# Building both long-convolution filters ahead of the projections of a one-core diffusion step, with their norm folded into the short convolution

## The reference, cut to what matters

```python
def _hyena_spectrum(n, w1, b1, w2, b2, w3, b3, freq):
    ...
    h = jnp.sin(fr * (z @ w1.astype(f32) + b1.astype(f32)))
    h = jnp.sin(fr * (h @ w2.astype(f32) + b2.astype(f32)))
    h = (h @ w3.astype(f32) + b3.astype(f32)).reshape(n, HY_ORDER, 2, HY_DIM)
    ...
    h = h * jnp.exp(-t01[:, None] * deltas[None, :])[:, None, None, :]
    ...
    filt2n = jnp.concatenate([h_fwd, jnp.zeros((1, HY_ORDER, HY_DIM), f32), h_bwd[:0:-1]], axis=0)
    filt2n = filt2n * lax.rsqrt(jnp.sum(filt2n * filt2n, axis=0, keepdims=True) + EPS)
    return jnp.fft.rfft(filt2n, axis=0)

def _hyena(u, conv_w, conv_b, spec, bias):
    n = u.shape[1]
    uc = _short_conv3(u, conv_w, conv_b)
    v, x1, x2 = jnp.split(uc, HY_ORDER + 1, axis=-1)
    ...
        return y + b_o.astype(jnp.float32) * zf
    z = x1.astype(jnp.float32) * long_conv(v, spec[:, 0], bias[0])
    z = x2.astype(jnp.float32) * long_conv(z, spec[:, 1], bias[1])
    return z.astype(u.dtype)
```

## Time and profile before

| what | value |
|---|---|
| runs | 928.21, 933.62, 936.93 us, median 933.62 |
| span of the profiled execution | 936.8 us (first to last instruction), 0.1 below the highest run |
| TensorE busy | 815.2 us, 87% |
| VectorE, ScalarE, GpSimd busy | 379.1, 272.2, 108.8 us |
| mean granted TensorE clock | 0.927 |
| input projection starts, `uT` ends | 75.3 us, 187.3 us |

### The profile page before, as it was taken

The page is one execution under the profiler, slowest core; times in us unless marked ns, Lnnn a source line. Parts: engine busy times, 40 slices in busy tenths (PEclk is TensorE's granted clock), DMA queues, the critical chain, the costliest instruction groups (busy, mean ns, idle before and its releaser), DMA issues.

```text
span 936.8 us, 11642 instructions
## 1 busy us (share of the span) xinstructions
PE 815.2 (87%) x4091; PEld 455.8 (49%) x4091; DVE 379.1 (40%) x848; ACT 272.2 (29%) x636; POOL 108.8 (12%) x161
## 2 busy tenths in 40 slices
PE   4779999999888996999977699988889998999860
PEld 0236665544443464555535346555554565555430
DVE  3366583265164143332111544654651432322114
ACT  1241212121451142122211536564540332222111
POOL 2300000000000003100013002202200022010120
PEclk9879999999988996899999799889999967999995
DMA  9991222259982246999997966202109378999965
GB/s 268 369 340 38 82 90 97 90 180 342 267 344 75 105 155 252 326 408 410 411 348 246 352 219 251 89 4 92 48 1 349 135 265 299 405 410 410 379 246 205
DMA packets 84559, 220.17 MB, mean 235 GB/s; under 512 B 9636, under 2 KB 19549, under 8 KB 84185
## 3 DMA queue, kind: packets, MB, share of 16 engines
q1 hardware_dynamic: 73570, 197.04, 58.3%
q0 software_dynamic: 9120, 18.75, 5.9%
q10 hardware_dynamic: 1816, 3.68, 1.1%
HBM read 214.77 MB, written 14.89 MB: 245 GB/s over the span
## 4 chain that ended last, share of the span: by engine, by line
PE 65%; DMA 15%; DVE 7%; ACT 4%; issue 4%; SPq 3%; DVEq 1%; POOLq 1%; POOL 0%; ACTq 0%
PE ps L903 58%; PE ps L910 4%; DMA ring<-in_moe_w_up_dram 3%; DMA ring<-in_w_mod_dram 2%; PE ps L1130 2%; DMA arena<-in_moe_w_up_dram 2%; DMA y_rows<-arena,ck 2%; SPq L643 2%; DMA xn<-y_rows 1%; DVEq L1877 1%; SPq L660 1%; DMA h_rows<-xn 1%; DMA hT<-h_rows,rows_in 1%; DVE negmax L1930 1%; ACT hT L1598 1%
## 5 line engine op out<-in xcount | busy, mean ns | idle before, releaser
L903 PE MATMUL ps<-arena 128*64 128x256 f32 (+12 forms) x1164 | 244.0, 455 | 26.2 <-DMA arena<-in_moe_w_up_dram 7.1
L903 PEld LDWEIGHTS ps<-arena 128*64 128x64 f32 (+4 forms) x1164 | 131.9, 172 | 119.2 <-issue 72.0
L903 PE MATMUL ps<-ring,hT 128*128 128x512 f32 (+2 forms) x384 | 134.1, 509 | 4.5 <-issue 3.9
L903 PE MATMUL ps<-ring,arena 128*64 128x256 f32 (+1 forms) x784 | 111.3, 431 | 4.8 <-DMA ring<-in_moe_w_down_dram 3.6
L903 PEld LDWEIGHTS ps<-ring,hT 128*128 128x128 f32 x384 | 73.3, 193 | 63.2 <-issue 58.8
L903 PEld LDWEIGHTS ps<-ring,arena 128*64 128x64 f32 x784 | 53.8, 137 | 50.6 <-issue 27.8
L910 PE MATMUL ps<-ident,arena 128*128 128x128 f32 (+2 forms) x332 | 52.3, 300 | 15.4 <-DVE hT L1936 3.6
L1554 ACT ACTIVATE arena<-ps 128x256 f32<-128x256 f32 (+4 forms) x88 | 38.5, 453 | 89.0 <-PE ps L903 84.9
L903 PE MATMUL ps<-hT,ring 128*128 128x384 f32 x192 | 62.1, 486 | 0.0
L2262 DVE TENSOR_TENSOR arena<-arena,ps 128x128 f32<-128x128 f32 x37 | 10.6, 287 | 125.3 <-ACT arena L1660 125.3
L903 PE MATMUL ps<-ring,condT 128*32 128x512 f32 x384 | 52.9, 676 | 9.7 <-DMA ring<-in_w_mod_dram 9.0
(11 more groups left out here) (299 smaller groups left out, 878.6 us busy)
## 6 DMA issues: line engine op xcount, KB each, us to landing
ring<-in_w_mod_dram SPq DMA_DIRECT2D x48, 1024.0 KB, 8.3
ring<-in_moe_w_down_dram SPq DMA_DIRECT2D x22, 1024.0 KB, 16.2
ring<-in_moe_w_gate_dram SPq DMA_DIRECT2D x38, 512.0 KB, 12.9
ring<-in_moe_w_up_dram SPq DMA_DIRECT2D x38, 512.0 KB, 15.1
arena<-in_moe_w_gate_dram SPq DMA_DIRECT2D x36, 512.0 KB, 8.7
arena<-in_moe_w_up_dram SPq DMA_DIRECT2D x36, 512.0 KB, 9.7
arena<-in_moe_w_down_dram SPq DMA_DIRECT2D x15, 1024.0 KB, 10.9
ring<-in_ev_w_in_dram SPq DMA_DIRECT2D x9, 1024.0 KB, 13.2
```

What stands on the lines that cost most here:

```text
L903: mm = pe.matmul(out, lhsT, rhs, **kw)
```

## The change

Both filters are built before chunk 2, and the steps that follow are put ahead of x's transposes. The scale 1/root is no longer put on the spectrum. The first filter's goes into the coefficients of the short convolution of v, the second's into those of x1, per channel and token group; for this the roots are transposed to channels on partitions (`root_turn`). The skip term becomes a tap: root times bias is added to row 0 of the filter before its transform (`bias_taps`). The energies have 32 output rows in place of 128, in one bank, the context's in one column group and the latents' in another. The four loads of the filter network's first layer go from ScalarE's queue to the head of SyncE's; the decay table is sent before piece 2 in place of piece 4, and the skip term is loaded for one partition in place of 128.

```diff
@@ banks
     B.stage("filt3.0", 2 * NT)
+    B.stage("filt3.1", 2 * NT)
     mod_stage("start", 2)
+    B.stage("energy0", 1)
+    B.stage("rootT0", 1)
+    B.stage("spec0", 2 * NT)
     mod_stage("start", 3)
-    B.stage("energy0", 2)
+    B.stage("energy1", 1)
+    B.stage("rootT1", 1)
+    B.stage("spec1", 2 * NT)
+    B.stage("convT", 1)
     B.stage("hT0.0", 6)
...
@@ buffers
-        filt = view(6144, NT, 2, HY)
+        filt = [view(6144, NT, 2, HY), view(16896, NT, 2, HY)]
...
+        raw = [flat_hT[:, D * (1 + i):D * (2 + i)].rearrange("p (r n) -> p r n", r=2) for i in range(2)]
@@ SyncE
                 if i == 0:
+                    load(sp, in_filt, zT, d["zT"])
+                    load(sp, in_filt, filtc[0:EMB, 3 + HID:3 + 2 * HID], d["ev_filt_w1"][0])
+                    load(sp, in_filt, filtc[:, 0:1], d["ev_filt_b1"].rearrange("a n -> n a"))
+                    load(sp, in_filt, filtc[:, 2:3], d["ev_filt_freq"].rearrange("a n -> n a"))
...
-                if i == 4:
                     load(sp, in_filt3, decay, d["decay"].rearrange("p (a b) -> p a b", b=HY))
-                    load(sp, in_filt3, hybias[:, 0, :], d["ev_hy_bias"][0, 0].partition_broadcast(P))
-                    load(sp, in_filt3, hybias[:, 1, :], d["ev_hy_bias"][0, 1].partition_broadcast(P))
+                    load(sp, in_filt3, hybias[0:1, :, :], d["ev_hy_bias"])
@@ TensorE
             def spectrum(od):
-                pe.wait_ge(esq_ready, (od + 1) * NT)
+                pe.wait_ge(tap_ready, od + 1)
...
+                bank = claim(f"energy{od}")
+                for t, r in ((0, 0), (1, 0), (0, 1), (1, 1), (2, 0), (2, 1)):
+                    pe.wait_ge(esq_ready, od * NT + max(t, 1) + 1)
+                    g = GRP[t]
+                    mm = product(bank[32 * g:32 * g + 32, :], onesm[:, 0:32], sqs[:, t, r, :], start=t < 2 and r == 0, stop=t != 1 and r == 1)
+                fill_inc(mm, f"energy{od}")
+
+            def root_turn(od):
+                pe.wait_ge(root_ready, od + 1)
+                bank = claim(f"rootT{od}")
+                for g in range(2):
+                    for c in range(NCH):
+                        at_col = 32 * (NCH * g + c)
+                        mm = pe.transpose(bank[:, at_col:at_col + 32], energy_root[od][:, g, c * P:(c + 1) * P], ident[0:32, 0:32])
+                fill_inc(mm, f"rootT{od}")
...
             filters(0)
-            for i in (2, 3, 4):
-                mod_step("start", i)
+            filters(1)
+            mod_step("start", 2)
             energies(0)
             loaded(pe, in_mod)
-            for t in range(NT):
-                mixer_turn(0, t)
+            root_turn(0)
             loaded(pe, in_dft)
             spectrum(0)
+            for i in (3, 4):
+                mod_step("start", i)
+            energies(1)
+            root_turn(1)
+            spectrum(1)
             bank = claim("convT")
...
+            for t in range(NT):
+                mixer_turn(0, t)
             for i in range(6):
                 drained_wait(pe, "hT0.0", i)
             for q in (6, 7, 8, 0, 1, 2, 3, 4, 5):
-                if q == 7:
-                    filters(1)
-                if q == 8:
-                    energies(1)
-                    spectrum(1)
-                if q == 0:
-                    pe.wait_ge(spec_done, 12)
@@ ScalarE
             def energy_roots(od):
+                bank = filled_wait(act, f"energy{od}")
                 for g in range(2):
-                    act.wait_ge(eroot, 2 * od + g + 1)
-                    act.activation(esc[:, g, :], esc[:, g, :], ACT.Sqrt).then_inc(escale_ready, 1)
+                    ins = act.activation(energy_root[od][:, g, :], bank[32 * g:32 * g + 32, :], ACT.Sqrt, bias=eps_col[0:32, :], scale=0.5)
+                drain_inc(ins, f"energy{od}")
+                act.drain().then_inc(root_ready, 1)
+
+            def spectrum_copies(od):
+                for i in (2, 4, 0):
+                    copy_out(f"spec{od}", i, H[:, od, i % 2, i // 2, :], bank_of(f"spec{od}", i)[:, :])
...
+            mod_step("start", 2)
+            energy_roots(0)
+            for t in range(NT):
+                filter_squares(1, t)
+            spectrum_copies(0)
+            mod_step("start", 3)
+            energy_roots(1)
             loaded(act, in_x)
             for t in range(NT):
                 norm_tile(0, t)
-            energy_roots(0)
+            spectrum_copies(1)
...
+                if m < 2 * NCH:
+                    for g, (a, b) in enumerate(((0, NPR), (NPR, T))):
+                        act.activation(uc[:, m, a:b], bank[:, a:b], ACT.Identity, bias=conv_scaled[:, g, 3, m:m + 1], scale=conv_scaled[:, g, 1, m:m + 1])
@@ VectorE
+            def bias_taps(od):
+
+                dve.wait_ge(root_ready, od + 1)
+                tap = raw[0][0:1, :, :]
+                dve.tensor_tensor(tap, energy_root[od][0:1, :, :], hybias[0:1, od, :].unsqueeze(1).broadcast_to([1, 2, HY]), ALU.mult)
+                settle()
+                first = filt[od][0:1, 0:2, 0, :]
+                dve.tensor_tensor(first, first, tap, ALU.add).then_inc(tap_ready, 1)
...
             filters(0)
+            filters(1)
+            bias_taps(0)
+            root_inverse(0)
+            for i in range(1, 3):
+                mod_step("start", i)
+            spectrum_copies(0)
+            bias_taps(1)
+            root_inverse(1)
             norm(0)
-            energies(0)
-            for i in range(1, 5):
-                mod_step("start", i)
+            mod_step("start", 3)
+            spectrum_copies(1)
+            mod_step("start", 4)
             for t in range(NT):
                 modulate_tile(0, 0, t, "hT0.0", 2 * t + 1)
-            spectrum(0)
...
-            filters(1)
-            energies(1)
-            spectrum(1)
```

More of the change, by code:

```diff
@@ L450, in build_step @@
         convraw = view(15360, P, parts=48)
-        esc = view(15488, 2, HY)
+        energy_root = [view(15488, 2, HY, parts=32), view(13312, 2, HY, parts=32)]
         hidden = view(16512, T, parts=HID + 1)
@@ L1288, in spectrum @@
                         for k in range(2):
-                            mm = product(bank[:, :], dfts[:, r, k, ft * P:(ft + 1) * P], filt[:, 1 + k, r, :],
+                            mm = product(bank[:, :], dfts[:, r, k, ft * P:(ft + 1) * P], filt[od][:, 1 + k, r, :],
                                            start=k == 0, stop=k == 1)
@@ L1293, in spectrum @@
                     bank = claim(f"spec{od}", r)
-                    mm = product(bank[:, :], dftp[:, r, :], filt[:, 0, r, :], start=True, stop=True)
+                    mm = product(bank[:, :], dftp[:, r, :], filt[od][:, 0, r, :], start=True, stop=True)
                     fill_inc(mm, f"spec{od}", r)
@@ L1782, in _ @@
                 modulate_tile(0, 0, t, "hT0.0", 2 * t)
-            heads_copy(0)
-            for t in range(NT):
-                filter_squares(1, t)
-            heads_copy(1)
-            energy_roots(1)
-            heads_copy(2)
+            for q in range(3):
+                heads_copy(q)
             act.wait_ge(qvar, 1)
@@ L2386, in energies @@
-            def energies(od):
-                for g in range(2):
-                    bank = filled_wait(dve, f"energy{od}", g)
-                    drain_inc(dve.tensor_scalar(esc[:, g, :], bank[:, :], 0.5, EPS, ALU.mult, ALU.add), f"energy{od}", g)
-                    dve.drain().then_inc(eroot, 1)
-            def spectrum(od):
-                for g in range(2):
-                    dve.wait_ge(escale_ready, 2 * od + g + 1)
-                    dve.reciprocal(esc[:, g, :], esc[:, g, :])
-                settle()
-                for i in range(2 * NT):
-                    ft, r = i // 2, i % 2
-                    bank = filled_wait(dve, f"spec{od}", i)
-                    ins = dve.tensor_tensor(H[:, od, r, ft, :], bank[:, :], esc[:, GRP[ft], :], ALU.mult)
-                    drain_inc(ins, f"spec{od}", i)
-                settle()
-                for ft in range(NT):
-                    dve.tensor_tensor(H[:, od, 0, ft, :], H[:, od, 0, ft, :], hybias[:, od, :], ALU.add)
-                dve.drain().then_inc(spec_done, 6)
@@ new lines, in root_inverse, with spectrum_copies @@
+            def root_inverse(od):
+                bank = filled_wait(dve, f"rootT{od}")
+                first = bank[:, 0:8 * 32].rearrange("p (g c k) -> p g c k", g=2, c=NCH)[:, :, :, 0]
+                drain_inc(dve.reciprocal(inv_root_c[:, :, NCH * od:NCH * od + NCH], first), f"rootT{od}")
+            def spectrum_copies(od):
+                for i in (3, 5, 1):
+                    bank = filled_wait(dve, f"spec{od}", i)
+                    drain_inc(dve.tensor_copy(H[:, od, i % 2, i // 2, :], bank[:, :]), f"spec{od}", i)
@@ L2413, in _ @@
                 modulate_tile(0, 0, t, "hT0.0", 2 * t + 1)
-            spectrum(0)
             bank = filled_wait(dve, "convT")
```

(4 more changed lines are left out.)

61 lines of the change are left out of this document (27 added, 34 removed).

## The result

The changed kernel takes 939.34 us (median of 20 runs, 935.81 to 943.8) against 933.67 for the kernel before (20 runs). The ratio is 1.0063, with a 95% interval of 1.0046 to 1.0079: 4.3 to 7.4 us slower. The forecast was 936.0, 2.4 above before, with 0.80 for a change of under 1% either way.

The account below looks back on a forecast made before the run. TensorE's timeline decides: holes until 63.78 us, gapless after. Loads, filters, energies, waits and tail put q = 6 at 93.4, plus 2.6 clock 96.0, against 93.6: 933.6 + 2.4 = 936.0 us; own range 932 to 940, wider 928 to 944.

Parts of the forecast that it names:

- q = 6: Start of the projection pieces ending with `uT`: forecast at 96.0 us, against 93.6 for no gain; `uT` ends 93.8 later.
- Loads: Start of kernel: four issues add 2.2 us, decay 1.9; piece 3 lands at 26.7, filters start at 28.6.
- The clock behind the holes: Both spectra: each new wait may start one at the low clock, costing 2.6 us; one of two counted.
- Filters at 1.2 GHz: Both filter builds on TensorE run at the low clock: 2 x 10.5 = 21.1 us, bounds 15.9 to 21.1.
- the wait: Between energies and spectrum, for roots and taps: 4.1 us uncovered, twice, 8.2 in all; bounds 3 to 5 each.
- The tail: Second spectrum's end at 87.1 to q = 6 at 93.4: last bank out, chunk 3 summed, twelve blocks modulated in 4.29 us.
- What costs nothing: Removed VectorE and ScalarE work, ScalarE's extra short-convolution operation, coefficients and ring: covered by TensorE, no time either way.
- the ring: Weight-piece buffers: piece 12 gets its place at 49.7 instead of 36.2, with over 20 us in hand, so no cost.
- rival 4: Short convolution: ScalarE's third operation comes onto TensorE's path, 2.4 us more, 938.4 us; chance 0.10.
- Rival 1: Clock stays low through chunk 2 and first energies, both spectra slowed: 9.7 us, q = 6 at 103.1, 943.1 us; chance 0.17.
- Rival 2: Second filter build runs at the high clock, VectorE paces, taps at 52.1: 927.9 or 925.3 us; chance 0.12.
- Rival 3: Second filter build fits the weights' holes (10.7 us), needing high clock and short waits: q = 6 at 80, 920 us; chance 0.05.

Follow-up runs that it names:

- the second comparison: Changed kernel, unedited, timed again against the kernel before on another chip: 936.46 us, ratio 1.0018 (0.9989 to 1.0047).
- the second pair of profiles: Kernel before and changed kernel, both unedited, each profiled once more; times 939.04 us (one run) and 936.46 us.
- e5: Kernel before with only the changed kernel's new load order, skip term still loaded for all partitions: 933.59 us, ratio 0.9994.
- e1: Changed kernel with seven throwaway products on TensorE in each of the two new waits: 934.21 us, ratio 0.9981 to the kernel before.
- e6: Changed kernel with eight throwaway products on TensorE ahead of chunk 1, before the filters: 930.0 us, ratio 0.9952 to the kernel before.
- e10: e3 with its two leftover holes closed, plus e6's eight throwaway products and four ahead of the first spectrum: 918.41 us, ratio 0.9802 to the kernel before.
- e2: Changed kernel with chunk 3's products moved from behind the first spectrum into the first wait: 933.26 us, ratio 0.9991 to the kernel before.
- e3: e2 with x's transposes moved into the second wait and the modulation beside the second spectrum: 928.82 us, ratio 0.9921 to the kernel before.
- e4: Kernel before, unchanged, run once for a second profile: 939.04 us.
- e9: Kernel before with only e6's eight throwaway products ahead of chunk 1: 933.17 us, ratio 0.9998.

## Why the prediction was right or wrong, point by point

**The range and the sign.** 939.34 lies in 928 to 944, slower as forecast, by 5.7 where 2.4 was said; the second comparison gave 1.9. The start alone gives 2.3 (189.7 against 187.4), or 2.8 by the second pair of profiles. Where the first comparison's further 3 us are from is not settled: two comparisons of the same two programs differ by 3.8, and the stages behind `uT` by up to 10 between profiles.

**q = 6 was forecast at 96.0 and came at 94.8; `uT` was to end at 189.8 and ended at 189.7.** This is closer than the steps deserve, and luck, since two errors of opposite sign cancel:

- *Loads: wrong.* Piece 3 was to land at 26.7, and the filters to start at 28.6. It landed at 22.9, filters at 24.8: 3.8 sooner, below even the lower bound of 26.4. I added 2.2 for four issues ahead of the first piece, and 1.9 for the decay. But e5 shows piece 3 only 1.2 later than before with both edits, and over all profiles that show its landing it is 22.9 to 23.9 with the new loads against 22.0 and 22.6 with the old. Which of the two terms was too large no run separates.
- *The clock behind the holes: right in kind, wrong in number.* I took one spectrum of two at 2.6. Both lost it (11.46 and 11.34 against 8.75), in both profiles. And I left out the third hole, the 3.60 ahead of q = 6, though my own tail had 6.3 us there: the 144 matmuls took 33.01, against 31.24 without a hole. Together 2.7 + 2.6 + 1.8 = 7.1 in place of 2.6. e1 settles the cause for the spectra.
- *Filters at 1.2 GHz: right,* 20.85 against 21.1. That was the term with most in it, and the one that went against the rule in the Trainium skill, "TensorE: Matmul & The Clock Gate", section "Why this matters for your kernels", by which gapless work brings the full clock. The trace does not agree with it here: 20.85 us without a gap at 1.2 GHz. e6 adds that in this place too, once other work has raised it, the level holds through the same matmuls, as it did at 85.76 in the earlier trace rows.
- *Chunk 2* 2.96 (2.9), *energies* 3.60 (3.5), *the wait* 4.08 and 4.04 (4.1), chunk 3 1.92 (1.85): right, from rows of another stage with another shape. One partition's 1024 elements cost 1.21 (1.25).
- *The tail* from the spectrum's end to q = 6 was 6.6 (6.3).
- *What costs nothing:* ScalarE's third operation, VectorE's reciprocals, the ring: `uT` kept its 62.08 and the last hole behind it its 0.19, so rival 4 is out.
- *Rival 1* (the clock low through the energies) did not occur: chunk 2 took 2.96 and the energies 3.60. *Rival 2* did not occur in the changed kernel, but e6 made it happen, and VectorE ended the taps at 49.1 where 52.1 was worked out with the later start of 28.6, so 23.8 behind the filters' start against 23.5. *Rival 3* needed the high level and short waits, as was said. e10 supplies the high level; its waits are not shorter (8.1 us from the end of the first energies to the spectrum, since VectorE is behind), but work stands in them. It starts q = 6 at 74.4 where 80 was worked out, and lands at 918.4 where 920 was.

**Where the expected gain went.** 18.3 us of the second filter did leave the stretch behind q = 6. But from the start of the filters to q = 6 it is 70.0 us (24.78 to 94.77), where it was 49.6 (25.69 to 75.29): 20.4 more. The old holes, 10.7, are gone from it, and the chunks take 1.9 less. In their place came 10.3 for the second filter's products, at the low level, where 5.3 had been paid at the high one; 11.3 for its spectrum, 2.6 of it clock; 8.1 of two waits that nothing covered; and 3.7 between x's transposes and q = 6. With the filters' start 0.9 earlier and 1.8 of clock behind q = 6 less 0.7 of small differences, that is the 2.3 by which `uT` ends later. Of the old holes about half (4.72 and 0.73) were waits for pieces and half (5.58) the wait for the modulation, behind chunk 3's way over DRAM. The change filled them, and opened its own. Its two waits come with the taps, that is, with the norm folded in: the spectrum before waited for squares only. No run builds the filters early and leaves the scale on the spectrum, so what each half of the change is worth by itself is open.

## What to carry to other kernels

Moving work from a full stretch into one with holes pays only for what fits the holes, and a new dependence between engines (product, root, tap, product) is a hole of its own: put independent work of the waiting engine between its two ends, here chunk 3 and the transposes. Price each hole on TensorE twice, for its length and for the low clock of what follows it, and count them all, the one in front of the long stage too. Before a long run of matmuls check at which level it starts; a few throwaway products in an idle spot ahead of it were worth 6.5 us here, and nothing measurable where the loads were the bound.

## What the runs showed of the hardware that was not expected

- 24 float32 matmuls of 65 rows ran gapless for 20.85 us at 1.2 GHz, and the same 24 in 10.57 at 2.4 GHz when 6.2 us of matmuls of 128 rows went ahead (e6). The kernel before shows both too: 10.61 and 5.32 for 12.
- What a wait costs in clock is not one number. A wait of 4.1 us with eight small transposes in it cost the 20 matmuls behind it 2.5 to 2.7 us in each of four instances (two profiles of the changed kernel), 1.8 in two more (the second waits of e2 and e6, 10.55), and nothing in four where throwaway products or real ones stood in it (e1's two, the first of e2 and of e3). The empty hole of 3.5 to 3.6 ahead of q = 6 cost 1.8 in four profiles and 2.9 in e1. Its length alone does not decide: in e3 the clock stayed at 1.00 through a hole of 2.45 in the spectrum, and behind the one of 2.00 in the earlier trace rows it was down to 0.50.
- With four small loads at the head of SyncE's queue the filter network's first layer started at 5.3 to 5.5 us in nine profiles, without them at 9.2 to 10.3 in three. The pieces behind them did not clearly move: TensorE started the second piece at 13.1 to 14.3 with them, and at 14.9, 14.3 and 13.0 without (the kernel before, e4 and e9).
